# Splitting the last conditioning piece of each layer in two and multiplying the expert gate's half in later

## What is computed

```python
def layer_step(x, mod, ...):
    sh1, sc1, g1, sh2, sc2, g2 = jnp.split(mod, 6, axis=-1)
    o, new = mix_layer(modulate(rmsnorm(x, n1), sh1, sc1), ...)   # attention A, B and a state-space scan, then w_out
    x = x + g1 * o
    x = x + g2 * hier_moe(modulate(rmsnorm(x, n2), sh2, sc2), ...)
    return x, new

for l in range(DEPTH):
    mod_ctx = (jax.nn.silu(c_ctx) @ w_ada[l] + b_ada[l])[None, None, :]   # 6 * 1024 columns
    mod_lat = (jax.nn.silu(c) @ w_ada[l] + b_ada[l])[:, None, :]
```

## Time and profile before

| what | value |
|---|---|
| time, median of 3 runs | 774.62 us (773.35 to 775.12) |
| profiled execution: its own time / its span | 772.99 us / 771.1 us |
| TensorE: matmul busy / weight load busy | 97% / 75% of the span |
| VectorE, ScalarE, GpSimd busy | 75%, 66%, 7% |
| DMA, mean over the span | 241 GB/s, 186.22 MB |
| longest lines on the chain that ended last | L916 23%, L945 12%, L1078 12% |

### The profile page before, as it was taken

The page is one execution under the profiler, slowest core; times in us unless marked ns, Lnnn a source line. Parts: engine busy times, 40 slices in busy tenths (PEclk is TensorE's granted clock), DMA queues, the critical chain, the costliest instruction groups (busy, mean ns, idle before and its releaser), DMA issues.

```text
span 771.1 us, 11078 instructions
## 1 busy us (share of the span) xinstructions
PE 745.3 (97%) x4068; PEld 580.2 (75%) x4068; DVE 581.1 (75%) x964; ACT 506.7 (66%) x842; POOL 50.4 (7%) x36
## 2 busy tenths in 40 slices
PE   9999999899999999999999999988999999999994
PEld 6557877458967888888878888845798888888884
DVE  4258386987566899999878746789767799998965
ACT  3048693484457877877655778457556787777854
POOL 0001342000000000000000134200000000000000
PEclk9999999999999999999999999999999999999998
DMA  9963034977338999999854203095831289999902
GB/s 350 423 273 110 14 123 153 425 269 299 110 117 357 365 363 365 376 368 346 332 221 179 82 27 130 9 400 201 318 119 56 70 329 381 373 365 369 377 27 85
DMA packets 34062, 186.22 MB, mean 241 GB/s; under 512 B 5200, under 2 KB 6608, under 8 KB 17104
## 3 DMA queue, kind: packets, MB, share of 16 engines
q1 hardware_dynamic: 34000, 185.42, 63.4%
HBM read 182.79 MB, written 2.62 MB: 240 GB/s over the span
## 4 chain that ended last, share of the span: by engine, by line
PE 76%; DVE 10%; ACT 7%; issue 4%; DMA 2%; SPq 1%; DVEq 0%; ACTq 0%
PE psum L916 23%; PE psum L945 12%; PE psum L1078 12%; PE psum L1280 5%; PE psum L1043 4%; PE psum L894 3%; PE psum L725 3%; PE psum L977 3%; DMA ring<-in_first 2%; DVE att L2352 1%; PE psum L1250 1%; PE psum L1148 1%; ACT split L1484 1%; PE psum L929 1%; PE psum L1162 1%
## 5 line engine op out<-in xcount | busy, mean ns | idle before, releaser
L2141 DVE TENSOR_TENSOR split<-ring,split 128x2048 fp32r<-128x2048 f32 x96 | 219.7, 2290 | 23.3 <-ACT split L1619 21.8
L1619 ACT CAST split<-ring 128x2048 fp32r<-128x2048 f32 x96 | 183.5, 1912 | 21.3 <-PE psum L945 14.7
L916 PE MATMUL psum<-split,y_hi 128*128 128x512 f32 x512 | 161.0, 395 | 0.0
L916 PEld LDWEIGHTS psum<-split,y_hi 128*128 128x128 f32 x512 | 93.6, 188 | 18.2
L916 PE MATMUL psum<-split,y_lo 128*128 128x512 f32 x256 | 100.1, 391 | 0.0
L1078 PE MATMUL psum<-ring_r,hT_hi 128*128 128x512 f32 x216 | 73.2, 393 | 0.0
L945 PE MATMUL psum<-split,hidT 128*128 128x512 f32 x256 | 69.6, 394 | 0.0
L945 PEld LDWEIGHTS psum<-split,hidT 128*128 128x128 f32 x256 | 47.3, 188 | 12.4 <-DVE hidT_lo L2146 2.7
L916 PEld LDWEIGHTS psum<-split,y_lo 128*128 128x128 f32 x256 | 48.0, 188 | 10.2
L2583 POOL TENSOR_TENSOR ud<-const,da_hi 128x1024 fp32r<-128x1024 f32 x12 | 27.3, 2293 | 390.6 <-DVE da_lo L2242 383.1
L1078 PEld LDWEIGHTS psum<-ring_r,hT_hi 128*128 128x128 f32 x216 | 40.0, 188 | 9.0 <-issue 0.8
(11 more groups left out here) (326 smaller groups left out, 1444.0 us busy)
## 6 DMA issues: line engine op xcount, KB each, us to landing
ring<-in_w_gu SPq DMA_DIRECT2D x64, 1024.0 KB, 5.6
ring<-in_w_ada SPq DMA_DIRECT2D x40, 1024.0 KB, 6.9
ring<-in_w_down SPq DMA_DIRECT2D x32, 1024.0 KB, 5.6
ring<-in_w_rows SPq DMA_DIRECT2D x12, 1024.0 KB, 5.1
ring<-in_w_out SPq DMA_DIRECT2D x8, 1024.0 KB, 5.3
ring<-in_first SPq DMA_DIRECT2D x7, 1024.0 KB, 17.1
ring<-in_w_xbc SPq DMA_DIRECT2D x8, 800.0 KB, 8.2
par<-in_par SPq DMA_DIRECT2D x1, 1728.0 KB, 15.9
```

The lines of the kernel that those rows point to most:

```text
L916: last = pe.matmul(dst, x[:, g, t, :], w[:, j, :], start=(t == 0 and i == 0), stop=(t == KD - 1 and i == 2))
L1619: act.copy(splits[unit_split(n)][:, 0, :], slot(key)).then_inc(raised("whi", l, p), 1)
L2141: tt(lo, slot(unit_key(l, p, n)), hi.bitcast(F32), ALU.subtract).then_inc(raised("wlo", l, p), 1)
```

## The change

The columns of the second scale and of the experts' gate are no longer one sum of eight pieces but two sums of four. For `t = 2` (now `sc2` alone) and `t = 3` (now `g2` alone) a piece holds 256 rows and 1024 columns, the same 1 MB, and is done in eight matmuls of 256 columns. Their banks are copied, turned and biased apart, with half the columns each.

The four pieces of `t = 2` stand at the end of the heads. The four of `t = 3` stand behind them: in layer 0 all four within the output projection (`IN_WOUT`), in layer 1 one within it, two behind the last router product and one before `logits`. In layer 0 the turn of `t = 3` stands behind the last router product, and the two first `ahead` pieces, which stood there, go to before `logits`. In layer 1 the turn of `t = 3` stands ahead of the fourth expert. The pieces of `t = 1` are spread wider over the heads, since `rest` has become shorter. The loads keep the order of use.

```diff
+def last_piece(t):
+    return KD - 1 if t < 2 else KD // 2 - 1
+
+IN_WOUT = ({(2, KD - 2): 0, (2, KD - 1): 1, (3, 4): 2, (3, 5): 3}, {(2, KD - 2): 0})
...
-    ada = [("ada", l, t, k) for t in (1, 2) for k in range(KD)]
+    ada = [("ada", l, t, k) for t in (1, 2, 3) for k in range(last_piece(t) + 1)]
...
-    rest = ada[burst:8] + [("ada_turn", l, 1)] + ada[8:14]
+    rest = ada[burst:8] + [("ada_turn", l, 1)] + ada[8:10]
...
-    s += ada[14:15] + [("o_split",)] + ada[15:] + [("wsplit", 1), ("wout",), ("router", KD - 3)]
-    s += [("norm", 1), ("router", KD - 2)] + [("hrow", m, 0) for m in range(TILES)] + [("router", KD - 1)] + ahead[:2]
-    s += [("raw",), ("hrow", 0, 1), ("token",), ("hrow", 1, 1), ("logits",)] + [("hshift", m, 0) for m in range(TILES)] + [("hrow", 2, 1)]
+    s += ada[10:11] + [("o_split",)] + ada[11:12] + [("wsplit", 1), ("wout",), ("router", KD - 3)]
+    s += [("norm", 1), ("router", KD - 2)] + [("hrow", m, 0) for m in range(TILES)] + [("router", KD - 1)]
+    s += ada[13:15] if l else [("ada_turn", l, 3)]
+    s += [("raw",), ("hrow", 0, 1), ("token",), ("hrow", 1, 1)] + (ada[15:] if l else ahead[:2])
+    s += [("logits",)] + [("hshift", m, 0) for m in range(TILES)] + [("hrow", 2, 1)]
...
-    if ahead:
-        at = experts.index(("gua", 0, 3))
-        experts[at:at] = [("ada_turn", l + 1, 0)]
+    at = experts.index(("gua", 0, 3))
+    experts[at:at] = [("ada_turn", l + 1, 0) if ahead else ("ada_turn", l, 3)]
...
-                pieces += [("wout", l, i) for i in (2, 3)]
+                pieces += [("wout", l, i) for i in (2, 3)] + [("ada", l, 3, k) for k in IN_WOUT[l].values()]
...
-                for q in range(4):
-                    last = pe.matmul(psum[32 * q:32 * q + 32, 7, :], silu_c[:, k, :], w[:, q * 512:(q + 1) * 512],
-                                     start=first_one, stop=(k == KD - 1), skip_group_check=True,
-                                     tile_position=(0, 32 * q))
...
+                    for i in range(2):
+                        for q in range(4):
+                            at = D * i + 256 * q
+                            last = pe.matmul(psum[32 * q:32 * q + 32, 7, 0:256], silu_c[:, 2 * k + i, :], w[:, at:at + 256],
+                                             start=(k == 0 and i == 0), stop=(k == last_piece(t) and i == 1),
+                                             skip_group_check=True, tile_position=(0, 32 * q))
...
-                for i in range(4):
+                for i in range(4 if t < 2 else 2):
                     last = pe.transpose(psum[:, 7, i * P:(i + 1) * P], ada_rows[:, i * P:(i + 1) * P], ident)
...
+                                if (n, c) in IN_WOUT[l]:
+                                    ada(l, 3, IN_WOUT[l][n, c])
...
+                        src = a["w_ada"][l, 2 * k * P:(2 * k + 2) * P, (t + 2) * D:(t + 3) * D].rearrange("(i p) n -> p i n", p=P)
+                        dst = dst.rearrange("p (i n) -> p i n", i=2)
...
-                    elif kind == "ada" and arg[2] == KD - 1:
+                    elif kind == "ada" and arg[2] == last_piece(arg[1]) or kind == "ada_turn" and arg == (0, 3):
                         ada(arg[0], arg[1])
```

More of the change, by code:

```diff
@@ L723, in ada @@
                     pe.wait_ge(*fill(key, 7))
-                for q in range(4):
-                    last = pe.matmul(psum[32 * q:32 * q + 32, 7, :], silu_c[:, k, :], w[:, q * 512:(q + 1) * 512],
-                                     start=first_one, stop=(k == KD - 1), skip_group_check=True,
-                                     tile_position=(0, 32 * q))
-                if k == KD - 1:
+                if t < 2:
+                    for q in range(4):
+                        last = pe.matmul(psum[32 * q:32 * q + 32, 7, :], silu_c[:, k, :], w[:, q * 512:(q + 1) * 512],
+                                         start=first_one, stop=(k == KD - 1), skip_group_check=True,
+                                         tile_position=(0, 32 * q))
+                else:
+                    for i in range(2):
+                        for q in range(4):
+                            at = D * i + 256 * q
+                            last = pe.matmul(psum[32 * q:32 * q + 32, 7, 0:256], silu_c[:, 2 * k + i, :], w[:, at:at + 256],
+                                             start=(k == 0 and i == 0), stop=(k == last_piece(t) and i == 1),
+                                             skip_group_check=True, tile_position=(0, 32 * q))
+                if k == last_piece(t):
                     last.then_inc(*filled(key))
@@ L1383, in load @@
                     t, k = at
-                    src = a["w_ada"][l, k * P:(k + 1) * P, t * PIECE:(t + 1) * PIECE]
+                    if t < 2:
+                        src = a["w_ada"][l, k * P:(k + 1) * P, t * PIECE:(t + 1) * PIECE]
+                    else:
+                        src = a["w_ada"][l, 2 * k * P:(2 * k + 2) * P, (t + 2) * D:(t + 3) * D].rearrange("(i p) n -> p i n", p=P)
+                        dst = dst.rearrange("p (i n) -> p i n", i=2)
                 elif kind == "xbc":
@@ L1468, in ada @@
                 act.wait_ge(*full(key))
-                src = bank(key)
-                act.copy(ada_rows, src).then_inc(*was_read(key))
+                n = 512 if t < 2 else 256
+                act.copy(ada_rows[:, 0:n], bank(key)[:, 0:n]).then_inc(*was_read(key))
             def out_hi(l, n):
@@ L1903, in ada @@
                 dve.wait_ge(*full(key))
[L1905 to L1908, removed]
+                n = 4 if t < 2 else 2
+                at = 4 * n * t if t < 2 else (t + 2) * KD
+                src = bank(key)[:, 0:n * P].rearrange("p (i q j) -> p q i j", i=n, q=4)[:, :, :, 0:2]
+                bias = pcol[:, l * N_PROW + R_BADA + at:l * N_PROW + R_BADA + at + 4 * n]
+                tt(mods[:, l, at:at + 4 * n, :].rearrange("p (q i) j -> p q i j", q=4), src,
+                   bias.rearrange("p (q i) -> p q i", q=4).unsqueeze(3).to_broadcast((P, 4, n, 2)), ALU.add).then_inc(*was_read(key))
                 dve.wait_ge(*taken(key))
-                if t != 1:
+                if t in (0, 2):
                     n = t // 2
```

## The result

The changed kernel takes 779.13 us (median of 4 runs, 778.39 to 780.95) beside 773.99 us for the kernel before on the same chip (4 runs, 772.72 to 775.12): ratio 1.0078, 95% interval 1.0062 to 1.0093. The forecast was 779.7 us, range 775.8 to 782.0. The profiled execution took 778.39 us with a span of 776.6 us; before it was 772.99 and 771.1.

A forecast was written before the change was run, and what follows sets the result against it. The prediction took DVE to bound the heads and PE the projection. Savings of 1.3 us in the heads against costs, chiefly 3.0 us each in layer 0's projection and layer 1's router, gave +5.1 us: 774.62 to 779.7 us, range 775.8 to 782.0.

The forecast's parts named there:

- Heads, layer 0: First scores to output projection, layer 0: two DVE waits go and `mods` leaves the limiting chain, 1.3 us saved.
- Heads, layer 1: First scores to output projection, layer 1: PE waits where the removed piece stood, so 0 us gained.
- Projection, layer 0: Output projection, layer 0: first new piece 0.1 us in PE's wait, other three 3.0 us; shorter turn saves 0.3 us.
- Projection, layer 1: Output projection, layer 1: one new piece in PE's wait costs 0.1 us; shorter turn saves 0.3 us, paid later.
- Router to logits: Last router product to logits: layer 0 pays 0.1 us for a copy; layer 1's three new pieces cost 3.0 us.
- list of signs: Expected observations, among them last router product to logits 4.3 us in layer 0 and 5.2 us in layer 1.
- Gather, experts, loads: After the logits: gather as before, loads hidden at cost 0, bias step in VectorE's expert work 0.1 us.
- rival 4: Layer 1's experts: their weights come late, +7 us, 781.7 us; chance 0.06.
- Rival 1: Heads: PE sets their pace, so all eight pieces give back 7.9 us, time 773.1 us; chance 0.10.
- rival 2: Layer 1's three pieces are hidden, +2.1 us, 776.7 us; chance 0.10.
- Rival 3: Heads: they give about half, 3 us instead of 1.3, so +3.4 us, 778.0 us; chance 0.12.
- Rival 5: Whole kernel: given and taken cancel, total unchanged near 774.6 us; chance 0.06.

## Why the prediction was right

Its direction and size came out, and so did its reading of which engine is late in which stretch, but for the end of the heads (above). The terms one by one:

- **Heads, layer 0:** -1.3 forecast, -1.19 measured. The forecast's three parts (0.34, 0.64 and 0.19 us) give 1.17; that I took 1.3 had no row behind it. DVE's waits of 0.34 and 0.64 us are gone from their places, and a new one of 0.39 us stands elsewhere. But `mods` still stands among the scalings and did not go behind them as I had said. Whether its 0.18 us cost anything there isn't shown: DVE waits 0.41 us for PE behind it, as it did in the kernel before. DVE in time, changed kernel, and the same wait before (second fence):

```profile
159.01 1.02 DVE L2377 TENSOR_REDUCE att<-psum 128x1 f32<-128x384 f32 x2 [0.39 <-PE psum L1242]
...
160.34 0.18 DVE L1932 TENSOR_TENSOR mods<-psum,pcol 128x32 f32<-128x32 f32 x1
...
162.46 1.02 DVE L2377 TENSOR_REDUCE att<-psum 128x1 f32<-128x384 f32 x2 [0.41 <-PE psum L1234]
```

```profile
163.71 1.02 DVE L2352 TENSOR_REDUCE att<-psum 128x1 f32<-128x384 f32 x2 [0.41 <-PE psum L1217]
```

- **Heads, layer 1:** 0 forecast, +0.20 measured (44.33 or 44.34 us in four of the five profiles with these steps, 44.01 in the fifth). PE's wait for the last scaling opened where the piece had stood (0.58 us for `hT` at 543.42), as forecast.
- **Projection, layer 0:** this term was mis-sized. Forecast: 0.1 for the piece in the gap, 3 x 1.0 and -0.3 for the shorter turn, +2.8. Measured: +3.42, with 0.13 for the gap's piece and 1.2 for each other one. The row I took the 1.00 us from the earlier trace rows gives the piece, not the entry and exit between wide matmuls.
- **Projection, layer 1:** -0.2 forecast, -0.04 measured. The waits of 0.80 us are gone in both layers.
- **Router to logits:** layer 0 +0.4 forecast (0.1 for the copy, 0.3 for the turn that is paid here) and +0.33 measured; layer 1 +3.0 and +3.11. The forecast's list of signs has only +0.1 for layer 0 (4.3 us), which its own sum contradicts.
- **Gather, experts, loads:** 0 forecast and +0.09 in each layer for the gather; +0.4 and +0.23 for layer 1's experts (0.3 for the turn, 0.1 for the bias step). The added loads were hidden: rival 4 put 2 us on that stretch.

The chain from scores to final sums was thus 1.1 us too short in my sum, half of it the projection's 0.6. An output transfer that happened to be 0.65 us shorter brought the profiled time back to my number (778.39 against 778.1). Part of the closeness is luck. The medians give +5.14 us where the recorded ratio gives 6.0, so by the ratio too the sum was short.

Rival 1 (the heads are PE's) falls by the 1.0 us that both layers' heads gave together for eight pieces, rival 2 (layer 1's pieces hidden) by the 3.11 us. Rival 3 (the heads give 3 us) falls too: no hidden gain turned up behind the clock fall in layer 1. Rival 5 was the matmul busy share's answer; one piece cost 1.2 us, 1.0, 0.4 or 0.1 in four places of one kernel family, so it falls. What stays open is how the 1.19 us of layer 0's heads divide between the number of pieces and their places.

## What to carry to other kernels

Price a moved step by the stretch it leaves and the stretch it enters: the same 1 us of PE work gave back 0.3 us or less under a DVE chain and cost 1.2 us in unbroken PE work, and 0.1 us in a wait. Put such work into waits that the trace shows, keep it in one group where it breaks a run of other matmuls, and count how many pieces a wait still holds (the third behind the ranking cost 0.86 us). When a step that hands a bank from PE to another engine and back is moved, check what is queued right behind it.

## What the runs showed of the hardware

- Going from the projection's matmuls (128 output rows, split operands) to a piece's (32 output rows, plain fp32) and back costs about 0.1 us each way: start to start 0.27 and 0.28 us instead of 0.17. A piece behind another also takes less than a single one (three 2.73 us, one 1.00). Merging three interruptions into one saved 0.67 us.
- Twice the weight loads for the same columns cost nothing that shows: 9.8 us more of PEld busy time, ratio 0.9998.
- The granted clock fell from 1.00 to 0.50 (2.4 to 1.2 GHz) for about 3 us in layer 1's heads in all seven profiles whose pieces stood at or near the changed places, and in one of the seven with the old places. In each PE had stood still for 1.2 to 2.2 us shortly before. It fell from 153.5 us on in the kernel where PE waited 3.61 us. But seven kernels had the old places and a wait of 1.4 us there, and six kept their clock. The same program can go either way: during layer 0's ranking it fell in four profiles of fourteen, in kernels whose code there is that of others where it did not fall, and made logits to gather 7.6 to 8.7 us instead of 6.0 to 6.1. One profile of a kernel is thus uncertain by 1 to 3 us, the size of this whole question, and stage times should be compared only where the clock column agrees.
